# All value matmuls of a sparse attention step in one piece at its end, with five turned tiles kept

## The chip, the cores and the metric

The kernel runs on one core of one Trainium2 chip. The metric is the device time of one execution in microseconds (us). The kernel before takes 2674.22 us (median of 3 runs, 2672.18 to 2682.71).

## What is computed

A decoder trunk of two layers over 512 tokens of width 1024, all in 32-bit floats. What matters here is the middle of each layer, where three branches are mixed; one of them is a sparse attention of 8 heads in 2 groups:

```python
y_a = _conv_module(z_conv, ...) @ conv_out[l]
y_b = _spatial_gating(z_sgu, ...) @ sgu_out[l]
y_c = _nsa(z_q, z_kv, z_ngate, ...) @ nsa_out[l]
g_a, g_b, g_c = jnp.split(jax.nn.sigmoid(z_merge), N_BRANCHES, axis=-1)
h = h + (g_a * y_a + g_b * y_b + g_c * y_c) @ w_out[l]
...
# in _nsa, per block of 128 queries:
p_c = _masked_softmax(s_c, m_c) * m_c          # 31 compressed keys
o_c = jnp.einsum('bghqn,bngd->bqghd', p_c, vc)
p_s = _masked_softmax(s_s, m_s)                # selected blocks
o_s = jnp.einsum('bghqm,bgqmd->bqghd', p_s, vs)
p_w = _masked_softmax(s_w, m_w)                # sliding window
o_w = jnp.einsum('bghqs,bsgd->bqghd', p_w, vw)
return gc[..., 0:1] * o_c + gc[..., 1:2] * o_s + gc[..., 2:3] * o_w
```

With 512 tokens every block is among the selected ones, so the selected and the window part are both plain causal attention over up to 512 keys.

## The kernel before

**Units.** Nearly all work of TensorE (PE) is in *units*: a product of one 1024x128 slice of weights with the 512 tokens, in three matmuls per 128 rows (high by high, high by low, low by high part; lines 706, 709 and 712). ScalarE (ACT) rounds the weights to the high part (`split`, called by `ahead` three units in advance), GpSimd (POOL) makes the low part (line 655), VectorE (DVE) takes the unit's result out of PSUM.

**Attention steps.** The sparse attention has 16 (pair of heads, block of 128 queries) combinations per layer, the *steps* s = 0 to 15. The query blocks of a pair come in the order 3, 0, 2, 1 (`COLS`), so a step sees 512, 128, 384 or 256 keys. Its small matmuls are laid between the matmuls of the merge units. In loop round i (`for i in range(1, NS + 1)`) PE does a branch unit (12 matmuls) and a gate unit (24), and after each second of these 36 matmuls it calls `attention(i, p)` with p = 0 to 17. I call two unit matmuls a *piece*, and a loop round a *round*. In round i these things are issued:

- the scores of step i, `scores((i, 0))` (selected part) and `scores((i, 1))` (window part), both into the same two PSUM banks pS, so the second waits until DVE has taken the first out (semaphore `s_out`);
- the *turned tiles* of step i-1: `turned(i - 1, g)` transposes four 128x128 blocks of probabilities into the one PSUM bank pT; ACT copies it to SBUF (`turned_out`) before the next turned tile may be written (`st_out`). A step has 5, 2, 4 or 3 groups g (`n`), the last of them the 31 compressed keys;
- the value matmuls `values(i - 1, g)`, which read the copied tile and accumulate in pO;
- in rounds 3, 4, 6 and 10 a sum over partitions for a norm (`middle`: q2, mean, var, q3), which uses pT too.

The pieces at which they stand are `TURN_AT`, `VALUE_AT` and `EXTRA_AT`. The turned tiles lie in a ring of two SBUF tiles (`sq`), so that the third copy waits for the value matmuls of the first (semaphore `pv`, line 1495).

**The other engines.** DVE takes scores out of PSUM with a running maximum (`maxes`), ACT makes exponentials (`exps`), DVE the weights (`weigh`), ACT (and from s = 8 partly DVE) multiplies them in (`weighted`); only then may step s be turned (`p_in`). Both engines go strictly in the order written in their own loops over i: ACT from line 1528, DVE from line 2164. In these loops stand also: the square roots of the norms (each needs another table of functions on ACT than the exponential), the copies `pair_high` and `o_st` of finished pairs (rounds 5, 9, 13), the depthwise convolution (`conv`, DVE, rounds 1 to 3) and `late_pair` (DVE, the norm of the next pairs' queries: a reciprocal and a product, at the end of rounds 2, 4 and 10).

Of the kernel before, what the change touches and what calls it, by code (L numbers as in the profile page):

```python
# [17 lines left out]
def trunk(nc, x, mem, norm_ffn1, ffn1_wi, ffn1_wo, norm_mix, w_in, conv_w, conv_b, conv_ln_g,  # L18
# [54 lines left out]
    with ctx:  # L73
# [90 lines left out]
        vt = vtok[:, :, :].rearrange("p a (g c) -> p a g c", g=4)  # L164
        pt = sq

# [25 lines left out]
        NS = PAIRS * TT  # L192
        RING = 2

# [16 lines left out]
        EXTRA = {3: "q2", 4: "mean", 6: "var", 10: "q3"}  # L211
        EXTRA_AT = {3: 4, 4: 4, 6: 5, 10: 3}
        order, seq = ["q1"], []
        for i in range(1, NS + 1):
# [3 lines left out]
            if i in EXTRA:  # L218
                order.append(EXTRA[i])
        TURN_AT = {2: (0, 3), 3: (0, 3, 6), 4: (0, 3, 6, 11), 5: (0, 3, 6, 10, 12)}  # L220
        VALUE_AT = {2: {8: (0, 1)}, 3: {8: (0, 1), 11: (2,)}, 4: {8: (0, 1), 16: (2, 3)},
                    5: {8: (0, 1), 14: (2, 3), 17: (4,)}}
        STEP = {key: n for n, key in enumerate(order)}
# [469 lines left out]
        def _(pe):  # L693
# [145 lines left out]
            for l in range(L):  # L839
# [141 lines left out]
                def values(s, g):  # L981

                    j, c = pair_col(s)
                    n = GRP[s, g]
                    pe.wait_ge(st_out, risen(st_out, l, STEP[s, g] + 1))
                    if n == 0:
                        pe.wait_ge(sg_out, risen(sg_out, l, TT))
                    elif s % TT == 0 and g == 0:

                        if j == 1:  # L990
                            pe.wait_ge(o_st, risen(o_st, l, 1))
                        else:
                            pe.wait_ge(c_l, risen(c_l, l, j))
                    all_of_step = entries(s)
                    for x, (b, k) in enumerate(groups(s)[g]):
                        for e in range(KVG):
                            at = slice((2 * x + e) * P, (2 * x + e + 1) * P)
                            o = pO[e * DH:(e + 1) * DH, c * P:(c + 1) * P]
                            if b < 2:
                                v, p = vt[:, k, 2 * b + e, 0:DH], pt[:, n % RING, at]  # L1000
                            else:
                                v, p = vcs[0:NCMP, e, 0:DH], pt[0:NCMP, n % RING, at]
                            last = mm(o, v, p, start=((b, k) == all_of_step[0]),  # L1003
                                      stop=((b, k) == all_of_step[-1]))
                    last.then_inc(pv, 1)
# [23 lines left out]
                def opening(p):  # L1029
# [10 lines left out]
                    if p == 13:  # L1040
                        scores((0, 1))

                def attention(i, p):
                    n = len(groups(i - 1))
                    if p in TURN_AT[n]:
                        turned(i - 1, TURN_AT[n].index(p))
                    elif i in EXTRA and p == 3 * EXTRA_AT[i]:
                        middle(EXTRA[i], {"q2": 8, "mean": 9, "var": 10, "q3": 11}[EXTRA[i]])
                    elif p in (1, 8):
                        if i < NS:  # L1050
                            scores((i, p // 8))
                    elif p == 16:
                        if i % TT == TT - 1 and f"c{i // TT + 1}" in SLOT:
                            scores(f"c{i // TT + 1}")
                    for g in VALUE_AT[n].get(p, ()):
                        values(i - 1, g)

# [199 lines left out]
        def _(act):  # L1257
# [134 lines left out]
            for l in range(L):  # L1392
# [97 lines left out]
                def turned_out(s, g):  # L1490

                    n = GRP[s, g]
                    act.wait_ge(st_mm, risen(st_mm, l, STEP[s, g] + 1))
                    if n >= RING:
                        act.wait_ge(pv, risen(pv, l, n - RING + 1))
                    rows = P if (s, g) != last_group(s) else NCMP
                    m = 2 * len(groups(s)[g]) * P
                    copy(pt[0:rows, n % RING, 0:m], pT[0:rows, 0:m]).then_inc(st_out, 1)

# [29 lines left out]
                for i in range(1, NS + 1):  # L1529
# [11 lines left out]
                    if i == 13:  # L1541
                        pair_high(2)
                    if i == 8:
                        turned_out(i - 1, 0)
                    ahead(l, branch_unit_of(i - 1))
                    if i != 8:
                        turned_out(i - 1, 0)
                    turned_out(i - 1, 1)
                    if i == 8:
                        conv_high(0)  # L1550
                    if i < NS:
                        exps(i, 0)
                        if i % TT == 0:
                            exps_c(i // TT)
                    if i == 8:
                        conv_high(1)
                    ahead(l, gate_unit(i + 1))
                    for g in range(2, min(n, 4)):
                        turned_out(i - 1, g)
                    if i < NS:  # L1560
                        exps(i, 1)
                    if i == 8:
                        conv_high(2)
                    for g in range(4, n):
                        turned_out(i - 1, g)
# [151 lines left out]
        def _(dve):  # L1717
# [133 lines left out]
            for l in range(L):  # L1851
# [311 lines left out]

                for i in range(1, NS + 1):
                    if i == 9:
                        pair_low(0)
                        pair_low(1)
                    if i == 13:
                        pair_low(2)
                    if i < NS:  # L2170
                        maxes(i, 0)
                    gate(i)
                    if i < 4:
# [222 lines left out]
```

## Time and profile before

| | |
|---|---|
| runs | 2672.18, 2674.22, 2682.71 us |
| the profiled execution | span 2674.3 us, granted TensorE clock 0.997; no time is known around the span |
| PE busy | 2633.2 us (98%) |
| DVE, ACT, POOL busy | 1404.5 us (53%), 1095.5 us (41%), 1230.6 us (46%) |
| rounds 1 to 16, layer 1 | from 553.7 us to 779.2 us of the span; PE 220.3, DVE 128.5, ACT 139.6 busy of 225.5 us |
| rounds 1 to 16, layer 2 | from 1877.9 us to 2104.9 us; PE 221.2, DVE 130.2, ACT 140.5 busy of 227.0 us |
| chain that ended last | PE 63%, issue 17%, POOL 9%, DVE 4%, ACT 3% |

A busy time is a union of the instructions' own spans. Matmuls overlap in the pipeline (one of 512 columns is shown with some 0.39 us and the next starts some 0.23 us later), so what a piece of work costs PE is read from starts to starts, not from durations. In rows of the time line, `[1.14 <-ACT prob L1261]` says that the engine sat idle for 1.14 us before the row, and what ended it.

### The profile page before, as it was taken

Reading aid. Unit: us, or ns where it says so; the run is one execution under the profiler, and the core shown is the slowest. Engines: PE = TensorE matmul, PEld = TensorE weight load, DVE = VectorE, ACT = ScalarE, POOL = GpSimd, SP = SyncE. Lnnn points to the kernel's source line nnn. Section 1 sums busy time; section 2 is a strip of 40 time slices with the busy share of each in tenths; the row PEclk is TensorE's granted clock in tenths of the full one; section 3 lists DMA queues with packets and bytes.
Section 4 is the critical chain, followed back from the end, with each engine's and each line's share of the span. In section 5 each row is a group of like instructions: output and inputs, shape, how many; then the busy total and the mean of one; then the engine's idle time right before and its main releaser. Section 6 shows DMA issues by size and latency. Waiting matters only on the chain.

```text
span 2674.3 us, 35749 instructions
## 1 busy us (share of the span) xinstructions
PE 2633.2 (98%) x12597; PEld 2110.3 (79%) x12597; DVE 1404.5 (53%) x1813; ACT 1095.5 (41%) x1674; POOL 1230.6 (46%) x616
## 2 busy tenths in 40 slices
PE   8999999999999999999999999999999999999999
PEld 6888878866778778888888888887667787788887
DVE  4343458966536544252553535698664364543433
ACT  5322242367644554222342222424675445532222
POOL 4443446762234334444444444477522353444443
PEclk9999999999999999999999999999999999999999
DMA  4334334322233223333333343333222332233332
GB/s 136 102 94 118 102 93 111 75 60 56 60 87 107 79 79 110 95 94 100 89 102 95 95 123 93 105 103 72 60 54 54 99 112 74 87 102 95 100 97 79
DMA packets 474694, 243.75 MB, mean 91 GB/s; under 512 B 41052, under 2 KB 466886, under 8 KB 474566
## 3 DMA queue, kind: packets, MB, share of 16 engines
q1 hardware_dynamic: 474542, 242.04, 32.1%
q8 instruction: 80, 1.31, 0.2%
q14 instruction: 48, 0.39, 0.0%
q10 hardware_dynamic: 24, 0.01, 0.0%
HBM read 237.79 MB, written 2.10 MB: 90 GB/s over the span
## 4 chain that ended last, share of the span: by engine, by line
PE 63%; issue 17%; POOL 9%; DVE 4%; POOLq 3%; ACT 3%; DMA 1%; DVEq 0%; ACTq 0%; SPq 0%
PE pg L706 19%; PE pg L709 18%; PE pg L712 18%; POOL wL L655 8%; PE pA L1003 1%; POOLq L682 1%; PE pA L828 1%; PE pA L950 1%; POOLq L684 1%; PE pg L733 1%; DVE convb L1893 1%; ACT wH L1261 1%; PE pg L1224 1%; PE pg L1222 1%; PE pg L1223 1%
## 5 line engine op out<-in xcount | busy, mean ns | idle before, releaser
L655 POOL TENSOR_TENSOR wL<-raw,wH 128x1024 fp32r<-128x1024 f32 (+1 forms) x472 | 1088.4, 2307 | 1410.2 <-ACT wH L1261 1406.5
L1261 ACT ACTIVATE wH<-raw 128x1024 fp32r<-128x1024 f32 (+1 forms) x472 | 477.6, 1012 | 1124.3 <-PE pg L712 962.5
L706 PE MATMUL pg<-gxH,wH 128*128 128x512 f32 (+1 forms) x2288 | 895.8, 392 | 1.0 <-DVE gxL L1743 0.5
L712 PE MATMUL pg<-gxH,wL 128*128 128x512 f32 (+1 forms) x2288 | 892.2, 390 | 0.0
L709 PE MATMUL pg<-gxL,wH 128*128 128x512 f32 (+1 forms) x2288 | 887.0, 388 | 0.0
L706 PEld LDWEIGHTS pg<-gxH,wH 128*128 128x128 f32 x2288 | 429.9, 188 | 100.2 <-issue 14.7
L712 PEld LDWEIGHTS pg<-gxH,wL 128*128 128x128 f32 x2288 | 429.9, 188 | 89.9 <-issue 4.4
L709 PEld LDWEIGHTS pg<-gxL,wH 128*128 128x128 f32 x2288 | 430.0, 188 | 87.1 <-issue 3.5
L706 PE MATMUL pg<-hH,wH 128*128 128x512 f32 x1008 | 400.0, 397 | 3.1 <-DVE hL L1794 3.1
L712 PE MATMUL pg<-hH,wL 128*128 128x512 f32 x1008 | 399.5, 396 | 0.0
L709 PE MATMUL pg<-hL,wH 128*128 128x512 f32 x1008 | 397.1, 394 | 0.0
L1775 DVE SCALAR_TENSOR_TENSOR xT<-pg,xT 128x512 f32<-128x512 f32 x112 | 77.2, 691 | 358.9 <-PE pg L712 358.6
L1787 DVE TENSOR_TENSOR tmp<-tmp,rstd 128x512 f32<-128x512 f32 x88 | 194.5, 2211 | 117.9 <-ACT tmp L1335 117.9
L1794 DVE TENSOR_TENSOR hL<-tmp,hH 128x512 f32 x88 | 190.2, 2161 | 90.6 <-ACT hH L1261 90.6
L709 PEld LDWEIGHTS pg<-hL,wH 128*128 128x128 f32 x1008 | 189.8, 188 | 51.0 <-issue 12.7
L706 PEld LDWEIGHTS pg<-hH,wH 128*128 128x128 f32 x1008 | 190.4, 189 | 43.0 <-DVE hL L1794 4.8
L712 PEld LDWEIGHTS pg<-hH,wL 128*128 128x128 f32 x1008 | 190.1, 189 | 36.3
L1785 DVE TENSOR_TENSOR tb<-pg,rstd 128x512 f32<-128x512 f32 x88 | 60.7, 690 | 125.4 <-PE pg L712 124.8
L1893 DVE SCALAR_TENSOR_TENSOR pA<-convb,par,pA 128x512 f32<-128x512 f32 x158 | 114.3, 752 | 7.4 <-issue 0.8
L1790 DVE TENSOR_TENSOR tmp<-pg,tmp 128x512 f32<-128x512 f32 x88 | 60.9, 692 | 100.0 <-PE pg L712 97.3
L1261 ACT ACTIVATE sq<-pA 128x512 f32<-128x512 f32 (+1 forms) x112 | 59.1, 528 | 101.4 <-PE pA L828 70.7
L683 POOL TENSOR_TENSOR convb<-convb,wsn 128x512 f32<-128x512 f32 x60 | 84.6, 1411 | 9.1 <-issue 0.4
(271 smaller groups left out, 2232.4 us busy)
## 6 DMA issues: line engine op xcount, KB each, us to landing
raw<-in_ffn_wi SPq DMA_DIRECT2D x352, 256.0 KB, 3.1
raw<-in_w_in SPq DMA_DIRECT2D x200, 256.0 KB, 3.3
raw<-in_ffn_wo SPq DMA_DIRECT2D x128, 256.0 KB, 3.0
raw<-in_ffn_wo SPq DMA_DIRECT2D x64, 192.0 KB, 2.5
raw<-in_xkv SPq DMA_DIRECT2D x32, 256.0 KB, 2.9
raw<-in_w_out SPq DMA_DIRECT2D x32, 256.0 KB, 3.0
raw<-in_sgu_out SPq DMA_DIRECT2D x32, 128.0 KB, 2.3
raw<-in_conv_out SPq DMA_DIRECT2D x32, 128.0 KB, 2.3
```

The lines of the kernel that those rows point to most:

```text
L655: pool.tensor_tensor(wL[:, s % 4, 0:n, :], raw[:, s % 2, 0:n, :], wH[:, s % 4, 0:n, :].bitcast(F32), ALU.subtract)\
L683: pool.tensor_tensor(o, o, term, ALU.add)
L706: mm(o, wH[:, s, k, :], rh(k), start=(k == 0), stop=False)
L709: mm(o, wH[:, s, k, :], rl(k), start=False, stop=False)
L712: last = mm(o, wL[:, s, k, :], rh(k), start=False, stop=(k == kt - 1))
L1261: return act.activation(o, i, ACT.Copy, **kw)
L1775: STT(xT[:, k, :], bank, by, xT[:, k, :], ALU.mult, ALU.add).then_inc(evac, 1)
L1785: TTt(tb[:, 0, :], bank, rstd[:, :], ALU.mult).then_inc(evac, 1)
L1787: TTt(sr, sil, rstd[:, :], ALU.mult)
L1790: TTt(hb, bank, sr, ALU.mult).then_inc(evac, 1)
L1794: TTt(hL[:, slot, :].rearrange(flat), hb, hH[:, slot, :].rearrange(flat).bitcast(F32), ALU.subtract).then_inc(hid_l, 1)
L1893: STT(to, cin[:, j, k:k + T], w, o, ALU.mult, ALU.add)
```

## The change

On PE, `values` of all groups of step i-1 now stand at the last piece (p = 17) of round i. Behind them, in the same piece, stand the first scores of step i+1, in the rounds where i+1 is at least 2 and not 4, 8 or 12 (`FIRST_SCORES_EARLY`); those of step 1 stand in the opening before round 1. In rounds 4, 8 and 12 the first scores stay at p = 1, and the second are at p = 9; in the others the second are at p = 6 (before: 8). The turned tiles stand later, and the extra sums at p = 14 or 11 (before: 12, 12, 15 and 9). The ring of two tiles is replaced by five tiles of their own, of which three are parameter tiles of other parts of the layer (`gbc`, `bbc`, `wsT`). On ACT, `exps(i, 0)` moves ahead of the first turned tile's copy where the first scores are early, and the copies are spread anew around `exps(i, 1)`. On DVE, `maxes(i, 0)` and `gate(i)` move ahead of `pair_low` in rounds 9 and 13.

```diff
-        pt = sq
+        pt = (sq[:, 0, :], sq[:, 1, :], gbc[:, :], bbc[:, :, :].rearrange("p g t -> p (g t)"),
+              wsT[:, :, :].rearrange("p g t -> p (g t)"))
...
-        RING = 2
+        FIRST_SCORES_EARLY = [i for i in range(2, NS) if i % TT]
...
-        EXTRA_AT = {3: 4, 4: 4, 6: 5, 10: 3}
+        EXTRA_AT = {3: 14, 4: 14, 6: 14, 10: 11}
...
-        TURN_AT = {2: (0, 3), 3: (0, 3, 6), 4: (0, 3, 6, 11), 5: (0, 3, 6, 10, 12)}
-        VALUE_AT = {2: {8: (0, 1)}, 3: {8: (0, 1), 11: (2,)}, 4: {8: (0, 1), 16: (2, 3)},
-                    5: {8: (0, 1), 14: (2, 3), 17: (4,)}}
+        TURN_AT = {2: (3, 8), 3: (3, 7, 11), 4: (2, 5, 8, 11), 5: (2, 5, 8, 11, 14)}
...
                     if p == 13:
                         scores((0, 1))
+                    if p == 22:
+                        scores((1, 0))
 
                 def attention(i, p):
                     n = len(groups(i - 1))
                     if p in TURN_AT[n]:
                         turned(i - 1, TURN_AT[n].index(p))
-                    elif i in EXTRA and p == 3 * EXTRA_AT[i]:
+                    elif i in EXTRA and p == EXTRA_AT[i]:
                         middle(EXTRA[i], {"q2": 8, "mean": 9, "var": 10, "q3": 11}[EXTRA[i]])
-                    elif p in (1, 8):
-                        if i < NS:
-                            scores((i, p // 8))
-                    elif p == 16:
-                        if i % TT == TT - 1 and f"c{i // TT + 1}" in SLOT:
-                            scores(f"c{i // TT + 1}")
-                    for g in VALUE_AT[n].get(p, ()):
-                        values(i - 1, g)
+                    elif p == 1 and i < NS and i > 1 and i not in FIRST_SCORES_EARLY:
+                        scores((i, 0))
+                    elif p == (9 if i % TT == 0 else 6) and i < NS:
+                        scores((i, 1))
+                    elif p == 16 and f"c{i // TT + 1}" in SLOT and i % TT == TT - 1:
+                        scores(f"c{i // TT + 1}")
+                    if p == 17:
+                        for g in range(n):
+                            values(i - 1, g)
+                        if i + 1 in FIRST_SCORES_EARLY:
+                            scores((i + 1, 0))
...
-                    if n >= RING:
-                        act.wait_ge(pv, risen(pv, l, n - RING + 1))
+                    if s and g == 0:
+                        act.wait_ge(pv, risen(pv, l, n))
...
-                    if i == 8:
-                        turned_out(i - 1, 0)
                     ahead(l, branch_unit_of(i - 1))
-                    if i != 8:
-                        turned_out(i - 1, 0)
-                    turned_out(i - 1, 1)
+                    if i < NS and i % TT:
+                        exps(i, 0)
+                    turned_out(i - 1, 0)
                     if i == 8:
                         conv_high(0)
-                    if i < NS:
+                    if i < NS and i % TT == 0:
                         exps(i, 0)
-                        if i % TT == 0:
-                            exps_c(i // TT)
+                        exps_c(i // TT)
+                    if n > 2:
+                        turned_out(i - 1, 1)
                     if i == 8:
                         conv_high(1)
                     ahead(l, gate_unit(i + 1))
-                    for g in range(2, min(n, 4)):
+                    for g in range(2 if n > 2 else 1, min(n, 3)):
                         turned_out(i - 1, g)
                     if i < NS:
                         exps(i, 1)
                     if i == 8:
                         conv_high(2)
-                    for g in range(4, n):
+                    for g in range(3, n):
                         turned_out(i - 1, g)
...
                 for i in range(1, NS + 1):
+                    if i < NS:
+                        maxes(i, 0)
+                    gate(i)
                     if i == 9:
                         pair_low(0)
                         pair_low(1)
                     if i == 13:
                         pair_low(2)
-                    if i < NS:
-                        maxes(i, 0)
-                    gate(i)
```

The order on TensorE at the end of round 1, layer 1, before: the value matmuls of step 0 read the ring `sq` and `vtok` (values) or `vcs` (values of the compressed keys). The `kT,qT` row is the second scores of step 1; `ident,pc` is a turned tile.

```order
L950 MATMUL pA<-kT,qT 128x128 x2
L1003 MATMUL pA<-sq,vtok 64x128 x8
...
L828 MATMUL pA<-ident,pc 31x128 x2
...
L1003 MATMUL pA<-sq,vtok 64x128 x8
...
L1003 MATMUL pA<-sq,vcs 64x128 x2
L706 MATMUL pg<-hH,wH 128x512
```

and of the change, the same place (its lines are numbered one less):

```order
L827 MATMUL pA<-ident,pc 31x128 x2
...
L711 MATMUL pg<-gxH,wL 128x512
L1002 MATMUL pA<-sq,vtok 64x128 x8
L1002 MATMUL pA<-gbc,vtok 64x128 x4
L1002 MATMUL pA<-bbc,vtok 64x128 x4
L1002 MATMUL pA<-wsT,vcs 64x128 x2
L949 MATMUL pA<-kT,qT 128x384 x2
L705 MATMUL pg<-hH,wH 128x512
```

Three blocks of value matmuls have become one, and the first scores of step 2 (384 keys) follow it.

The order on ScalarE in round 5, before: `qT<-pA` is the copy `o_st`, `wH<-raw` an `ahead`, `sq<-pA` the copy of a turned tile, `prob,dn<-prob,nb` an exponential of step 5.

```order
L1261 ACTIVATE qT<-pA 128x512
L1261 ACTIVATE wH<-raw 128x1024
L1261 ACTIVATE sq<-pA 128x512 x2
L1477 ACTIVATE prob,dn<-prob,nb 128x128 x2
L1261 ACTIVATE wH<-raw 128x512
L1261 ACTIVATE sq<-pA 128x512 x2
L1477 ACTIVATE prob,dn<-prob,nb 128x128 x2
```

and of the change:

```order
L1265 ACTIVATE qT<-pA 128x512
L1265 ACTIVATE wH<-raw 128x1024
L1481 ACTIVATE prob,dn<-prob,nb 128x128 x2
L1265 ACTIVATE sq<-pA 128x512 x2
L1265 ACTIVATE wH<-raw 128x512
L1265 ACTIVATE gbc<-pA 128x512
L1481 ACTIVATE prob,dn<-prob,nb 128x128 x2
```

The first exponential now stands ahead of the copies of the turned tiles 0 and 1, and the copy of tile 3 has gone behind the second exponential.

## Rows read from the trace of the kernel before

**Rows 1.** Who waited for whom, TensorE, whole run: us, times, longest

```profile
PE pA L828 <- ACT prob L1261: 5.3, 4, 2.0
PE pA L828 <- ACT sq L1261: 5.1, 7, 1.1
```

**Rows 2.** Time line, PE, a score block (at 556.51): start us, us, line

```profile
556.18 0.40 PE L706 MATMUL pg<-hH,wH 128*128 128x512 f32 x1
...
556.93 0.50 PE L709 MATMUL pg<-hL,wH 128*128 128x512 f32 x1
557.27 0.40 PE L712 MATMUL pg<-hH,wL 128*128 128x512 f32 x1
557.50 0.40 PE L706 MATMUL pg<-hH,wH 128*128 128x512 f32 x1
```

**Rows 3.** Time line, PE, scores and eight value matmuls joined

```profile
561.51 0.39 PE L712 MATMUL pg<-gxH,wL 128*128 128x512 f32 x1
...
562.25 1.09 PE L1003 MATMUL pA<-sq,vtok 128*64 128x128 f32 x16
563.27 0.50 PE L706 MATMUL pg<-gxH,wH 128*128 128x512 f32 x1
```

**Rows 4.** Time line, PE, eight value matmuls (566.91), then two alone

```profile
566.58 0.40 PE L712 MATMUL pg<-gxH,wL 128*128 128x512 f32 x1
...
567.93 0.50 PE L706 MATMUL pg<-gxH,wH 128*128 128x512 f32 x1
...
569.19 0.40 PE L712 MATMUL pg<-gxH,wL 128*128 128x512 f32 x1
569.52 0.43 PE L1003 MATMUL pA<-sq,vcs 31*64 31x128 f32 x4
569.88 0.50 PE L706 MATMUL pg<-hH,wH 128*128 128x512 f32 x1
```

**Rows 5.** Time line, round 1 of layer 1: its start, then DVE, then ACT

```profile
553.74 0.39 PE L706 MATMUL pg<-hH,wH 128*128 128x512 f32 x1
...
558.96 0.69 DVE L1727 TENSOR_TENSOR tb<-pg,rstd 128x512 f32<-128x512 f32 x1
...
559.18 0.60 ACT L1261 ACTIVATE sq<-pA 128x512 f32<-128x512 f32 x1 [0.75 <-PE pA L828]
...
559.67 0.39 ACT L1477 ACTIVATE prob<-prob,nb 128x128 f32<-128x128 f32 x1
```

**Rows 6.** Time line, round 5 of layer 1: start, POOL and DVE

```profile
613.73 0.39 PE L706 MATMUL pg<-hH,wH 128*128 128x512 f32 x1
...
615.55 2.40 POOL L655 TENSOR_TENSOR wL<-raw,wH 128x1024 fp32r<-128x1024 f32 x1 [6.10 <-ACT wH L1261]
...
615.95 2.55 DVE L2151 SCALAR_TENSOR_TENSOR qT<-qT,g,rv 128x512 f32<-128x512 f32 x1
...
618.72 0.06 DVE L2058 MEMSET nb<- 128x2 f32 x1 [0.23 <-issue]
```

**Rows 7.** Time line, round 11 of layer 1: start, and DVE

```profile
699.42 0.39 PE L706 MATMUL pg<-hH,wH 128*128 128x512 f32 x1
...
700.74 3.35 DVE L2149 RECIPROCAL rv<-rv 128x512 f32<-128x512 f32 x1 [2.81 <-ACT rv L1571]
...
705.15 0.06 DVE L2058 MEMSET nb<- 128x2 f32 x1 [0.23 <-PE pA L828]
```

**Rows 8.** Time line, rounds 7 and 9: two late turned tiles, a table load

```profile
645.07 0.66 PE L828 MATMUL pA<-ident,prob 128*128 128x128 f32 x4 [0.84 <-ACT sq L1261]
...
646.38 1.28 ACT L1477 ACT_TABLE_LOAD   x1
...
675.06 0.66 PE L828 MATMUL pA<-ident,prob 128*128 128x128 f32 x4 [0.42 <-ACT sq L1261]
```

**Rows 9.** Time line, PE, the longest wait, in layer 2

```profile
1880.52 1.09 PE L828 MATMUL pA<-ident,prob 128*128 128x128 f32 x4 [2.00 <-ACT prob L1261]
```

**Rows 10.** Busy time by stretch: PE, PEld, DVE, ACT, POOL, PEclk, DMA, GB/s

```profile
1880.40:1884.40 4.00, 3.88 (x14) 2.85 (x15) 3.34 (x12) 2.06 (x3) 3.71 (x4) 0.57 0.06 17
```

More of the change, by code:

```diff
@@ L999, in values @@
                             if b < 2:
-                                v, p = vt[:, k, 2 * b + e, 0:DH], pt[:, n % RING, at]
+                                v, p = vt[:, k, 2 * b + e, 0:DH], pt[g][:, at]
                             else:
-                                v, p = vcs[0:NCMP, e, 0:DH], pt[0:NCMP, n % RING, at]
+                                v, p = vcs[0:NCMP, e, 0:DH], pt[g][0:NCMP, at]
                             last = mm(o, v, p, start=((b, k) == all_of_step[0]),
@@ L1493, in turned_out @@
                     act.wait_ge(st_mm, risen(st_mm, l, STEP[s, g] + 1))
-                    if n >= RING:
-                        act.wait_ge(pv, risen(pv, l, n - RING + 1))
+                    if s and g == 0:
+                        act.wait_ge(pv, risen(pv, l, n))
                     rows = P if (s, g) != last_group(s) else NCMP
                     m = 2 * len(groups(s)[g]) * P
-                    copy(pt[0:rows, n % RING, 0:m], pT[0:rows, 0:m]).then_inc(st_out, 1)
+                    copy(pt[g][0:rows, 0:m], pT[0:rows, 0:m]).then_inc(st_out, 1)
                 def pair_high(j):
```

## Prediction, made before the changed kernel ran

> **What bounds the kernel now.** I read the page first: TensorE is busy for 98% of the span, and in the two stretches of sparse attention for 220.3 of 225.5 us and 221.2 of 227.0 us. So what the change is worth is what it does to TensorE's own stream there: what its small blocks cost, and where it stands still. Then I read who TensorE waits for: 11 times for ACT in front of a turned tile, 10.4 us in all [rows 1], four times for the weighted probabilities and seven times for the copy of the tile before. Then the time line, from starts to starts, for the price of a block; and last the time lines of ACT and DVE around the places where the new order puts one thing behind another. ACT and DVE are busy for some 60% of these stretches: they bound nothing by their sums, but both work in a strict order, and TensorE waits for single results.
>
> **Price of the blocks.** Two unit matmuls start 0.23 us apart; a score block of 128 columns makes 0.75 between its neighbours, and the next distance 0.34 [rows 2]. So it costs 0.75 + 0.34 - 2 x 0.23 = 0.63 us. In the same way eight value matmuls alone cost 1.35 + 0.11 - 0.23 = 1.23, and two alone (compressed keys) 0.69 + 0.11 - 0.23 = 0.57 [rows 4]; that is 0.11 per matmul and 0.35 for being a block. Scores and eight value matmuls joined cost 1.76 + 0.11 - 0.23 = 1.64 [rows 3] where apart they would cost 0.63 + 1.23 = 1.86: joining two blocks of unlike shape saves 0.22, of like shape 0.35.
>
> Now the count, per layer. Steps of five tiles (four of them): three value blocks become one, saving 0.35 + 0.22 each, 2.3 in all; the join with scores only changes its side. Steps of three tiles (four): the compressed block is joined, 0.9. Steps of two tiles: all three were joined before, nothing. Steps of four tiles: value blocks are joined, but the joins with the scores (four) and with the compressed scores (three) go, -0.1. Sum 3.1 per layer, **-6.2 us** for both. That scores *behind* values are as cheap as values behind scores no row shows; at 22 places that may be 0.22 more or less each, so -1.4 to -11.
>
> **What goes with the old waits.** In the change every step's first turned tile stands two or three pieces later (0.46 us each), and the second scores in most rounds two pieces earlier, so the weighted probabilities come in time. The waits of [rows 1] go, 10.4 us, and with each some 0.16 more, since the matmul ahead is shown as busy for 0.39 while its successor would start after 0.23: 11 x 0.16 = 1.8. After the wait of 2.00 us [rows 9] the granted clock was 0.57 over 4.0 us [rows 10], TensorE partly at its 1.2 GHz level: 0.43 x 4.0 = 1.7 us of work lost, which goes too. Sum **-13.9 us**. (The ring's waits on ACT, for value matmuls, go as well; no wait of TensorE shows them as its cause.)
>
> **What comes.** The step that decides is on ACT: `exps(i, 0)` now stands ahead of the first copy `turned_out(i-1, 0)`. So the second turned tile, at p = 5 in rounds with four or five tiles, waits not only for the copy, but for all that the first exponential waits for: DVE's `maxes(i, 0)`, and what stands ahead of that on DVE. In the kernel before, the first two copies stood ahead of that exponential, and the second tile waited for the first copy alone. TensorE comes to the second tile six pieces and a turned tile (I take 0.4; four transposes are under the 0.63 of a score block) after the round's start: 6 x 0.46 + 0.4 = 3.2 us. Behind its wait is the whole stream, all units included, so each late tile is a loss in full.
>
> - Round 1. It starts at 553.74 [rows 5], in the change 0.63 later, since the first scores of step 1 have moved ahead of it: 554.4; the second tile is due at 557.6. DVE is without a gap there (it has the norm branch's low parts, the compressed weights and then the convolution to do), so its maximum is done at 558.96 as before [rows 5]; then two exponentials (0.39 each, 0.9 with their sums) and the copy, 0.60 [rows 5]: ready at 560.5. Wait 2.9, before the last tile a second one, since the fourth copy now stands behind `exps(1, 1)`, which waits for DVE's convolution: between 0 and 2, I take 1.2. In layer 2 the first tile is later too (2.00 us of idle time [rows 9]), 0.5 more. Both layers: 8.7.
> - Round 5. DVE begins the maximum at 618.72, behind `late_pair(2)`, 5.0 us after the round's start [rows 6]. Nothing in round 4 frees DVE earlier, and the round begins about where it did (the score block of 0.63 has moved ahead of it, some waits and joins have gone). The maximum takes 0.6, the exponentials 0.9, the copy 0.6: ready 7.1 us after the start, due at 3.2. Wait 3.8, in both layers 7.6.
> - Round 11. ACT's square root for the last queries ends when DVE's reciprocal starts, 1.3 us after the round's start, and the maximum begins at 5.7 [rows 7]. In the change the round's start is later by the score block of 256 keys (about 0.8), the second scores of round 10 stand 0.9 earlier, but the sum q3 0.9 later and on DVE's path: I put the chain 0.9 earlier against the round, maximum at 4.8. With 1.0 for it, 1.1 for the exponentials (256 columns) and 0.6 for the copy: 7.5, due at 3.2. Wait 4.2, both layers 8.4.
> - Round 7. The second tile was 0.84 + 0.16 = 1.0 late, behind the square root [rows 8]. Now the table load of 1.28 [rows 8] and the exponentials (1.1) come ahead of the copy, and the chain is 1.7 earlier against the round (0.8 and 0.9 as above): 1.7, both layers 3.4.
> - Round 9. 0.42 + 0.16 = 0.6 late before [rows 8], behind the copies of finished pairs; now 0.9 more for the exponentials, and 0.2 more because `pair_high(1)` waits for value matmuls that stand at the end of round 8: 1.7, both layers 3.4.
> - Round 3, by the same count (behind `late_pair(1)`): 0.2, both layers 0.4. In rounds 2, 6, 10 and 14 the second tile stands at p = 8, 1.4 later; in rounds 13 and 15 nothing long stands ahead of the maximum, and I count 2.7 to 3.1 against 3.2: nothing, but with little to spare.
>
> Sum **+31.9 us**. Bounds: if ACT's order hid all of it (the exponentials ready at once), 0; if every chain were as late as in the kernel before, with no gain from the earlier scores, some 8 more.
>
> **The clock.** Six of these waits are of 3 us and more (rounds 1, 5, 11, twice). One of 2.00 cost 1.7 us of clock [rows 9, 10]; waits of 1.1 in [rows 1] cost none. I take four falls, **+6.8 us**; bounds 0 and 10.2. The Trainium skill ("TensorE: Matmul & The Clock Gate", HAM oscillation) says that recurring idle stretches throw the engine back to its low clock each time; [rows 9, 10] agree once. By that rule it is six falls and 2696 us.
>
> DVE's product in `late_pair(2)` takes 2.55 us beside POOL's low part [rows 6]; a product of the same size in [rows 5] takes 0.69. The skill ("GPSIMD Engine Reference", Key points) has the two engines share their ways into SBUF, with contention for instructions of two SBUF inputs. The trace agrees; and as ACT's `ahead` starts POOL at the same time in the change, I keep 2.55. Were it free of POOL, 3.7 us less in both layers.
>
> **Sum.** -6.2 - 13.9 + 31.9 + 6.8 = +18.6 us on the profiled execution's span of 2674.3 (0.1 from the median): 2692.9, rounded to **2693 us**. Its own range is 2683 to 2701.
>
> **Rivals.**
> 1. *The order on ACT does not bind* (faster). For it: ACT has 40% idle time, and the first scores are issued at the end of the round before, so that the maximum could be early. Against it: the rows of rounds 5 and 11, where DVE is behind a reciprocal of 3.35. Then there are only the gains, and perhaps 4 us of waits: 2674.3 - 6.2 - 13.9 + 4 = 2658.
> 2. *The new waits are half as long and leave the clock alone* (no change). For it: a round that was delayed gives ACT and DVE time to run ahead in the next. Against: the chains start anew in each round. 2674.3 - 20.1 + 16 = 2670, and up to 2685 with waits of 24 and four falls.
> 3. *More falls and later chains* (slower still): six falls, 8 us more of waits: 2704.
>
> **How the numbers follow.** My forecast 0.50, rival 1 0.13, rival 2 0.29, rival 3 0.08. What a measurement can tell from no change is about 0.5%, 13.4 us: faster is under 2661, slower over 2687.6. Slower: nine tenths of mine and rival 3, 0.53; faster: rival 1, 0.13; same 0.34. The range of eight in ten leaves out most of rival 1 and the far end of rival 3: 2663 to 2703.
>
> **What would show it.** The value matmuls in one row per round, with scores behind them. TensorE's waits for `prob` near 0 except in layer 2's round 1; its waits for the copies (now into `sq`) some 25 us in all, the longest about 4, at the second turned tile of rounds 1, 5, 7, 9 and 11; behind them stretches with a clock under 1. Wrong would be: waits for copies of the size of before, or a clock of 1.00 behind the long ones; or the joined piece costing more than 0.11 per matmul and 0.35 + 0.13 + its scores.

## The result, and the profile after

The changed kernel took 2697.11 us (median of 4 runs, 2693.58 to 2697.84), the kernel before 2674.91 beside it: ratio 1.0073, 95% interval [1.0061, 1.0086]. So it is 22 us slower; forecast were 2693 us. In the profiled executions the spans are 2695.1 and 2674.3 us, 20.8 apart.

Who waited for whom in the changed kernel, TensorE, whole run (us in total, times, longest), against [rows 1]; the copy is line 1265 now, the turned tile 827:

```profile
PE pA L827 <- ACT sq L1265: 27.7, 12, 4.3
...
PE pA L827 <- ACT bbc L1265: 0.3, 1, 0.3
...
PE pA L827 <- ACT prob L1265: 0.2, 1, 0.2
```

The waits for the weighted probabilities (`prob`) are gone but for 0.2 us, and those for the copies (`sq`) are 27.7 us. Where they stand, in layer 1 (time line of TensorE; the number in brackets is the idle time ahead): rounds 1, 5, 7, 9 and 11, each time the second turned tile (one of 0.18 in round 3 is left out):

```profile
560.74 1.11 PE L827 MATMUL pA<-ident,prob 128*128 128x128 f32 x4 [2.90 <-ACT sq L1265]
...
623.59 0.65 PE L827 MATMUL pA<-ident,prob 128*128 128x128 f32 x4 [3.86 <-ACT sq L1265]
...
653.69 0.55 PE L827 MATMUL pA<-ident,prob 128*128 128x128 f32 x3 [1.45 <-ACT sq L1265]
...
682.49 0.55 PE L827 MATMUL pA<-ident,prob 128*128 128x128 f32 x3 [0.73 <-ACT sq L1265]
...
713.85 0.69 PE L827 MATMUL pA<-ident,prob 128*128 128x128 f32 x2 [4.27 <-ACT sq L1265]
```

The chain in front of the longest kind, round 5, which answers to [rows 6] (time line, PE, POOL, DVE and ACT):

```profile
616.24 0.50 PE L705 MATMUL pg<-hH,wH 128*128 128x512 f32 x1
...
618.03 2.38 POOL L654 TENSOR_TENSOR wL<-raw,wH 128x1024 fp32r<-128x1024 f32 x1 [6.35 <-ACT wH L1265]
618.44 2.52 DVE L2154 SCALAR_TENSOR_TENSOR qT<-qT,g,rv 128x512 f32<-128x512 f32 x1
...
621.19 0.06 DVE L2061 MEMSET nb<- 128x2 f32 x1 [0.23 <-issue]
...
621.91 0.40 ACT L1481 ACTIVATE prob<-prob,nb 128x128 f32<-128x128 f32 x1 [3.95 <-DVE nb L2064]
...
622.94 0.60 ACT L1265 ACTIVATE sq<-pA 128x512 f32<-128x512 f32 x1 [0.16 <-issue]
```

Read it backwards from the tile at 623.59: it waits for the copy at 622.94, this stands behind the exponential, which ACT could not start for 3.95 us, since DVE began the maximum at 621.19, behind the product. In the kernel before the two copies were made at 615.38 and 617.27, ahead of all this. The maximum is 4.95 us behind the round's start (5.0 before).

Granted clock, by stretch (columns as in [rows 10]; PEclk is the eighth number, after POOL): six stretches in the attention steps at half clock.

```profile
559.90:566.90 7.00, 6.16 (x21) 4.65 (x22) 6.56 (x11) 2.37 (x6) 6.39 (x5) 0.51 0.14 40
624.90:628.30 3.40, 3.40 (x13) 2.65 (x12) 2.44 (x8) 0.62 (x2) 1.28 (x1) 0.50 0.07 22
713.60:717.00 3.40, 3.15 (x11) 1.86 (x11) 0.00 (x0) 1.31 (x3) 0.81 (x1) 0.50 0.00 0
1894.60:1898.00 3.40, 3.40 (x12) 2.77 (x11) 3.33 (x2) 0.77 (x2) 3.26 (x2) 0.50 0.00 0
1956.10:1959.50 3.40, 3.40 (x12) 2.33 (x11) 1.08 (x6) 1.11 (x2) 1.27 (x1) 0.50 0.00 0
2044.80:2051.60 6.80, 5.60 (x18) 3.80 (x19) 2.13 (x7) 2.11 (x5) 1.26 (x1) 0.50 0.16 46
```

That is 27.3 us with TensorE at its 1.2 GHz level, behind each of the six waits of 2.9 us and more; before it was the one stretch of [rows 10]. Half of such a stretch is lost where TensorE works: 13.7 us, or 12.6 without the 2.2 us in which it stood still anyway, against 1.7 before.

The joined block (round 1's end, against [rows 3, 4]):

```profile
571.04 0.40 PE L711 MATMUL pg<-gxH,wL 128*128 128x512 f32 x1
571.37 1.09 PE L1002 MATMUL pA<-sq,vtok 128*64 128x128 f32 x16
572.29 0.60 PE L1002 MATMUL pA<-gbc,vtok 128*64 128x128 f32 x8
572.73 0.60 PE L1002 MATMUL pA<-bbc,vtok 128*64 128x128 f32 x8
573.26 0.43 PE L1002 MATMUL pA<-wsT,vcs 31*64 31x128 f32 x4
573.63 0.92 PE L949 MATMUL pA<-kT,qT 64*128 64x384 f32 x4
574.47 0.50 PE L705 MATMUL pg<-hH,wH 128*128 128x512 f32 x1
574.81 0.39 PE L708 MATMUL pg<-hL,wH 128*128 128x512 f32 x1
```

By the working of the prediction it costs 3.43 + 0.34 - 2 x 0.23 = 3.31 us.

**A balance for every run.** From each profile I take the span, TensorE's waits of over 0.15 us in the two attention stretches, all time at half clock up to TensorE's last matmul (the last 4 us of a span have none, so a slow clock costs nothing there), and what is left: span - waits - half of the time at half clock. (A wait that lies in a slow stretch is taken off one and a half times; for the changed kernel, three of whose waits reach into a slow stretch by 0.7, 0.3 and 1.2 us, the rest is 1.1 us too low, for the others by 0.7 at most.)

| kernel | median, us | ratio, 95% | span | waits | at half clock (in attention) | rest |
|---|---|---|---|---|---|---|
| before | 2674.91 | 1 | 2674.3 | 10.9 | 13.7 (3.4) | 2656.6 |
| changed | 2697.11 | 1.0073 [1.0061, 1.0086] | 2695.1 | 28.3 | 37.5 (27.3) | 2648.1 |
| second tile later | 2684.15 | 1.0024 [1.0014, 1.0034] | 2682.4 | 16.7 | 30.7 (23.9) | 2650.3 |
| one copy first | 2679.03 | 1.0007 [0.9998, 1.0016] | 2677.3 | 17.7 | 20.5 (10.2) | 2649.4 |
| copies first, rounds 5, 11 | 2678.88 | 1.0014 [1.0005, 1.0024] | 2675.4 | 17.6 | 17.1 (10.2) | 2649.3 |
| two copies first | 2675.32 | 0.9998 [0.9986, 1.0009] | 2676.6 | 16.9 | 23.9 (6.8) | 2647.7 |
| late pairs behind | 2674.32 | 0.9996 [0.9987, 1.0005] | 2672.1 | 14.2 | 13.7 (10.2) | 2651.1 |
| both | 2670.49 | 0.9978 [0.9969, 0.9987] | 2668.4 | 11.3 | 13.7 (6.8) | 2650.3 |
| + fourth copy | 2665.10 | 0.9955 [0.9941, 0.9969] | 2662.4 | 8.4 | 10.2 (0) | 2649.0 |
| values apart | 2673.28 | 0.9980 [0.9970, 0.9991] | 2664.8 | 7.3 | 0 (0) | 2657.6 |
| first scores in their round | 2669.11 | 0.9972 [0.9960, 0.9984] | 2664.0 | 7.7 | 3.4 (0) | 2654.6 |
| scores ahead of values | 2663.41 | 0.9952 [0.9937, 0.9967] | 2658.1 | 7.7 | 0 (0) | 2650.4 |
| convolution later | 2660.99 | 0.9940 [0.9928, 0.9952] | 2656.8 | 3.3 | 10.2 (0) | 2648.4 |

The last column is what to see: 2648 to 2651 wherever the value matmuls are joined with each other and with early scores, 2657 to 2658 where they stand apart, and 2654.6 in the one kernel that joins them but leaves the first scores in their round. The differences beyond that are waits and clock.

### The profile page after: what moved, and what is told of

The parts are those of the page before. It is cut to its first block, busy times and chain, and to the rows that moved or that the text cites. A ratio compares the mean times of both kernels' runs of the same rounds, so it can differ in the third digit from the quotient of the medians.

```text
span 2695.1 us, 35671 instructions
## 1 busy us (share of the span) xinstructions
PE 2637.2 (98%) x12597; PEld 2119.6 (79%) x12597; DVE 1401.6 (52%) x1813; ACT 1096.3 (41%) x1674; POOL 1230.8 (46%) x616
## 4 chain that ended last, share of the span: by engine, by line
PE 63%; issue 17%; POOL 9%; DVE 4%; ACT 3%; POOLq 3%; DVEq 1%; DMA 1%; ACTq 0%; SPq 0%
PE pg L705 18%; PE pg L711 18%; PE pg L708 18%; POOL wL L654 8%; PE pA L827 2%; PE pA L1002 1%; POOLq L681 1%; PE pA L949 1%; POOLq L683 1%; PE pg L732 1%; ACT prob L1481 1%; ACT wH L1265 1%; PE pg L1228 1%; PE pg L1226 1%; PE pg L1227 1%
## 5 line engine op out<-in xcount | busy, mean ns | idle before, releaser
L827 PE MATMUL pA<-ident,prob 128*128 128x128 f32 x416 | 65.5, 284 | 30.6 <-ACT sq L1265 27.7
L827 PEld LDWEIGHTS pA<-ident,prob 128*128 128x128 f32 x416 | 52.6, 146 | 49.2 <-ACT sq L1265 32.8
```

The costliest lines, as they stand in the source:

```text
L827: return pe.transpose(dst, src, ident[0:k, 0:k])
```

## The experiments

All start from the changed kernel; each was timed together with the kernel before, which gave medians of 2675.7 (runs 1 to 4), 2676.1 (5 to 8) and 2677.4 (9 to 11); so the ratios in the table are the surer numbers. In the expectations theory A says that a wait is the end of a strict chain on ACT and DVE less the tile's due time; B, C and D are the rivals named in them.

**1. Two copies first (ACT).** In rounds with first scores early, the edit in short (the line that made the second copy further down leaves it out there):

```diff
-                    if i < NS and i % TT:
-                        exps(i, 0)
                     turned_out(i - 1, 0)
+                    if i < NS and i % TT:
+                        if n > 3:
+                            turned_out(i - 1, 1)
+                        exps(i, 0)
```

> The changed kernel, with ACT's order of the kernel before at one place: in rounds 1 to 15 (without 4, 8, 12) the copies of turned tile 0 (and of tile 1 where there are four or five tiles) stand ahead of exps(i, 0). Theory A (the second turned tile is late because its predecessor's copy stands behind an exponential that waits for DVE): the six waits per layer (27.7 us over the run) go but for some 3 us at later tiles, and the eight 3.4 us windows of half clock in the attention stretches go with them; 2697 - 25 - 13 = 2659 us, faster than the kernel before by 14 to 18. Theory B (it is the joined piece at the round's end that makes ACT and DVE late, whatever their order): the waits stay above 15 us and the time above 2685.

Measured: 2675.32, 22 us better than the changed kernel and level with the kernel before, but 16 short of what I expected. The waits at the second tile are gone but for 0.4 to 0.9 us in round 1. In their place stand two others, one for the copy before the last tile in round 1, one for DVE's eviction in front of the second scores (rounds 5 and 11). Waits of TensorE in layer 1's stretch (the third and fourth copies go into `gbc` and `bbc`):

```profile
PE pA L827 <- ACT bbc L1265: 4.4, 1, 4.4
PE pA L949 <- DVE nb L2069: 2.8, 2, 1.5
PE pA L827 <- ACT sq L1265: 0.4, 1, 0.4
PE pA L827 <- ACT gbc L1265: 0.3, 1, 0.3
```

Their causes, on the time lines of DVE and ACT of the same run, round 1:

```profile
558.95 6.80 DVE L1901 SCALAR_TENSOR_TENSOR convb<-convb,par 128x512 f32<-128x512 f32 x4
...
565.85 0.06 DVE L2066 MEMSET nb<- 128x2 f32 x1
...
566.58 0.40 ACT L1481 ACTIVATE prob<-prob,nb 128x128 f32<-128x128 f32 x1 [5.07 <-DVE nb L2069]
...
567.55 0.60 ACT L1265 ACTIVATE bbc<-pA 128x512 f32<-128x512 f32 x1
...
568.21 0.41 PE L827 MATMUL pA<-ident,pc 128*31 128x128 f32 x2 [4.35 <-ACT bbc L1265]
```

The fourth copy stands behind `exps(1, 1)`, and this behind four steps of DVE's convolution. In the changed kernel TensorE came to the last tile later, held up by its second and at half clock, and the same copy was in time. My expectation had let the late tile vanish and nothing else come due earlier.

**2. One copy first.** As 1, but `exps(i, 0)` directly behind the first copy.

> As e1, but only the copy of turned tile 0 stands ahead of exps(i, 0); that of tile 1 stays behind it. Theory A: the wait moves from the second to the third turned tile, which is due three pieces and a tile later (1.8 us, and in rounds 5 and 11 a score block later still, 2.6): rounds 5 and 11 keep some 1.5 us each per layer, rounds 1, 7 and 9 next to nothing; 2662 to 2668 us. Theory B: as the changed kernel, above 2685.

Measured: 2679.03, 11 above the upper end of what I expected, as run 1 was above its own. The wait that I had put at the third tile of rounds 5 and 11 did not come; the waits are those of run 1, with 0.7 more at the last tile of round 8 in each layer. Near run 1 and not near the changed kernel, so the first copy decides.

**3. Copies first in rounds 5 and 11 alone.**

> As e1, but in rounds 5 and 11 alone. Theory A: the waits of 3.9 and 4.3 us there go in both layers (16.7 us) with the five windows of half clock behind them (8 us), the others stay: 2697 - 25 + 2 = 2674 us, level with the kernel before. Theory B: above 2690.

Measured: 2678.88, 5 above what I expected; waits 17.6 against 28.3, slow stretches 10.2 against 27.3 us. What is left is mostly round 1 (2.9 and 3.1), the eviction, and 1.5 in round 7 of each layer.

**4. The late pairs behind (DVE).** ACT as in the changed kernel, but the reciprocals no longer stand ahead of the maximum:

```diff
-                    if i == 4:
-                        late_pair(2)
 ...
                         squared(1)
+                        late_pair(2)
 ...
                     gate(i)
+                    if i == 11:
+                        late_pair(3)
 ...
-                    if i == 10:
-                        late_pair(3)
```

> The changed kernel, ACT's order untouched; on DVE the query norm late_pair(2) moves from the end of round 4 to the end of round 5, and late_pair(3) from the end of round 10 to behind the gate of round 11, so that the first maximum of rounds 5 and 11 does not stand behind a reciprocal of 3.35 us. Theory A: the wait of round 5 goes (3.9 and 4.3 us), that of round 11 falls from 4.3 to about 1.5, since the square root and the table load on ACT remain; with the clock windows 2697 - 13 - 7 = 2677 us. A rival within A, that ACT itself is late there and not DVE: the waits stay at 3 us or more, 2690 us or more.

Measured: 2674.32. One cause was taken away on another engine, and the same waits went: round 5's wholly, round 11's from 4.27 to 1.10. In layer 1:

```profile
PE pA L827 <- ACT sq L1265: 6.6, 5, 2.9
```

Runs 1 to 4 settle the mechanism: an order on ACT and an order on DVE each bring the same waits or take them away. Theory B, by which these edits would leave the time above 2685, is refuted.

**5. Both.** Runs 1 and 4 together.

> Both edits of the first four runs: the copies of tiles 0 and 1 ahead of exps(i, 0) on ACT, and the two late reciprocals behind the convolution's squares (round 5) and the gate (round 11) on DVE. Theory A (the time is block prices + TensorE's waits + clock falls, and each wait is set by the strict order on ACT or DVE): copies first left 4.35 us at the last tile of round 1 (its copy stands behind exps(1, 1), that behind DVE's convolution) and 1.3 to 1.7 us in front of the second scores of rounds 5 and 11 (DVE evicts the first scores late, behind the reciprocal). The second kind goes, 6.0 us over both layers: 2669. Rival D (the lateness is only moved to the next chain, since DVE has the same work to do): 2675, as copies first alone.

Measured: 2670.49, as theory A had it (2669). The eviction is no longer waited for, and next to nothing has come in its place (one wait of 0.3 a layer).

**6. The fourth copy as well.** In round 1 it stands ahead of `exps(1, 1)`.

```diff
-                    for g in range(2 if n > 2 else 1, min(n, 3)):
+                    third = 4 if i == 1 else 3
+                    for g in range(2 if n > 2 else 1, min(n, third)):
```

> As the run with both edits, and in round 1 the fourth copy (third index) ahead of exps(1, 1) as well. Theory A: the wait of 4.35 us at the last tile of round 1 goes in both layers (8.7) and the two clock falls behind it (2 x 1.7): 2669 - 12 = 2657, faster than the kernel before by 18. Rival D: the last tile or the value matmuls wait for something else in its place, 2667 to 2670.

Measured: 2665.10, so 5 us and not 12. The waits of 4.1 and 4.3 and the slow stretches behind them are gone, but six smaller waits have come. Layer 1:

```profile
PE pA L949 <- DVE nb L2070: 1.6, 1, 1.6
PE pA L827 <- ACT prob L1265: 0.7, 1, 0.7
PE pA L827 <- ACT gbc L1265: 0.6, 2, 0.3
PE pA L827 <- ACT sq L1265: 0.4, 1, 0.4
PE pA L1002 <- ACT wsT L1265: 0.4, 1, 0.4
```

The first two stand in round 2, behind the same convolution. Rival D was half right: DVE's chain was late by itself, and the wait had only covered it. (The time, 2665, lies between theory A's 2657 and rival D's 2667.)

**7. Values apart.** As run 6, with the value matmuls in two or three blocks again:

```diff
+        VALUE_AT = {2: {17: (0, 1)}, 3: {14: (0, 1), 17: (2,)}, 4: {13: (0, 1), 17: (2, 3)},
+                    5: {12: (0, 1), 15: (2, 3), 17: (4,)}}
 ...
-                    if p == 17:
-                        for g in range(n):
-                            values(i - 1, g)
+                    for g in VALUE_AT[n].get(p, ()):
+                        values(i - 1, g)
+                    if p == 17:
```

> As the run with the fourth copy, but the value matmuls stand apart again (pairs 0-1 and 2-3 at pieces 12 and 15 of rounds with five tiles, 13 and 17 with four, 14 and 17 with three; what is left at piece 17). Prices the joining itself. By the blocks' prices as the two traces show them (0.35 per block, 0.2 per join with a block of unlike shape) the joins lost are worth 4.6 us a layer: 9 us above the run with the fourth copy, about 2666. By the prediction's own prices, 5.6 a layer, 11 us above. Rival (joining is worth nothing by itself, only the waits matter): within 2 us of it.

Measured: 2673.28, 8.2 above run 6; by the rests of the two profiles 8.6. Joining is worth what the prices of blocks say, but only where no wait takes it back.

**8. Scores ahead of the values** at a round's end.

```diff
+                        if i + 1 in FIRST_SCORES_EARLY:
+                            scores((i + 1, 0))
                         for g in range(n):
                             values(i - 1, g)
-                        if i + 1 in FIRST_SCORES_EARLY:
-                            scores((i + 1, 0))
```

> As the run with the fourth copy, but at the end of a round the next step's first scores stand ahead of the value matmuls and not behind them. Tells whether the order of the joined shapes has a price: the prediction left 0.22 us at 22 places open to both sides. If not: within 2 us of the run with the fourth copy (the maximum starts up to 3 us earlier, which no wait needs any more). If scores behind values are dear: 5 us faster; if they are cheap: 5 us slower.

Measured: 2663.41, within 2 us of run 6, so scores behind values are neither dear nor cheap. The same block as above, with the order reversed (time line, PE):

```profile
567.87 0.39 PE L711 MATMUL pg<-gxH,wL 128*128 128x512 f32 x1
568.19 0.92 PE L949 MATMUL pA<-kT,qT 64*128 64x384 f32 x4
569.03 1.09 PE L1002 MATMUL pA<-sq,vtok 128*64 128x128 f32 x16
569.96 0.61 PE L1002 MATMUL pA<-gbc,vtok 128*64 128x128 f32 x8
570.39 0.61 PE L1002 MATMUL pA<-bbc,vtok 128*64 128x128 f32 x8
570.93 0.43 PE L1002 MATMUL pA<-wsT,vcs 31*64 31x128 f32 x4
571.30 0.50 PE L705 MATMUL pg<-hH,wH 128*128 128x512 f32 x1
```

From 567.87 to 571.30 are 3.43 us, as in the changed kernel from 571.04 to 574.47: the order has no price. That closes the widest bound of the prediction's first term.

**9. The second tile later (TensorE alone).** ACT and DVE as in the changed kernel:

```diff
-        TURN_AT = {2: (3, 8), 3: (3, 7, 11), 4: (2, 5, 8, 11), 5: (2, 5, 8, 11, 14)}
+        TURN_AT = {2: (3, 8), 3: (3, 7, 11), 4: (2, 8, 11, 13), 5: (2, 8, 10, 12, 14)}
```

> The changed kernel, ACT's and DVE's orders untouched; only TensorE's order moves: in rounds with four or five tiles the second turned tile stands at piece 8 and not 5 (later ones at 11 and 13, or 10, 12 and 14). The wait is the chain's end less the due time, so it must shrink by three pieces, 3 x 0.46 = 1.4 us, where it is longer than that. Theory A: rounds 1, 5, 11 go from 2.9, 3.9 and 4.3 to 1.5, 2.5 and 2.9, round 7 to 0.1, round 9 to 0: 6.4 us a layer, 12.7 in all, and two to four of the eight clock windows: 2697 - 12.7 - 5 = 2679. Rival D (the copies behind each other are the limit; the wait goes over to the third tile, now only two or three pieces behind): 2688 to 2693.

Measured: 2684.15, between theory A's 2679 and rival D's 2688. The waits shrank by 11.6 us, against 12.7 expected, but they are others now; so the single waits that I had put at the second tile (1.5, 2.5 and 2.9) did not come. Layer 1:

```profile
PE pA L949 <- DVE nb L2064: 4.5, 3, 1.9
PE pA L827 <- ACT bbc L1265: 3.9, 1, 3.9
PE pA L1010 <- ACT bbc L1265: 0.5, 1, 0.5
```

The second scores (piece 6) now are the first to meet the late chain of rounds 5 and 11, and in round 1 it is the last tile. And the time at half clock hardly fell, 27.3 to 23.9 us: that is the 5 us that I missed by. The shorter waits at the second scores (1.8 to 2.2 us) were each followed by a slow stretch too.

**10. First scores in their round.** As run 6, with `FIRST_SCORES_EARLY` empty and `scores((1, 0))` at piece 1.

> As the run with the fourth copy, but a step's first scores stand at piece 1 of its own round again, none behind the value matmuls of the round before. Prices the move of the scores. By the blocks' prices 22 joins with the value matmuls are lost, 0.2 each: +4.6 us, and the maxima come 1 us later, for which no tile waits while the copies stand first: 2665 + 5 = 2670. Rival (the early scores matter for the second exponentials and the weighted probabilities, as in the kernel before, which waited four times for them): 2675 and more.

Measured: 2669.11, 4.0 above run 6, in the rests 5.7, where the prices of the joins give 4.6; the rival (2675 and more) does not hold. Behind ACT's repaired order the early scores bring their join and nothing besides.

**11. The convolution later (DVE).** As run 8, and round 1 does two convolution steps at each of two places where it did four; round 3 does the rest.

```diff
                     if i < 4:
-                        conv(4)
+                        conv(4 if i > 1 else 2)
 ...
                         squares(qT[:, 2, :])
-                        conv(4)
+                        conv(2)
```

> As the run with the scores ahead of the values, and four of the convolution's steps that DVE did in round 1 (two ahead of its second maximum, two at its end) are left to round 3. In that run TensorE still waits 1.0 us in round 1 for a copy behind an exponential, and 0.6 and 1.5 us in round 2 for DVE to evict the first scores, behind the convolution. Theory A: the latter go, about 3 us over both layers, little comes back in round 3: 2660. Rival D: round 3's sum over the convolution is late by as much (four steps, 5 us), and the time is the same or worse, 2663 to 2668.

Measured: 2660.99, ratio 0.9940 [0.9928, 0.9952] to the kernel before: the fastest of all, 16 us under the kernel before that was timed beside it and 36 under the changed one. That it is 2.4 under run 8 the times alone do not show (the intervals overlap); the profiles do, with waits of 3.3 us for 7.7. TensorE waits for nothing in round 3: it had room. What TensorE still waits for in layer 1's stretch:

```profile
PE pA L827 <- ACT gbc L1265: 0.9, 3, 0.3
PE pA L827 <- ACT sq L1265: 0.4, 1, 0.4
```

## Why the prediction was right, term by term

- **Blocks: -6.2 forecast, -7.1 measured** (the rest 2656.6 before, 2649.5 as the mean of the nine joined kernels with early scores other than the changed one, 2647.7 to 2651.1; the changed kernel itself, without its 1.1, gives -7.4). So the term is right within what these rests can tell. The bound's cause, a price for scores behind values, is refuted by run 8. One unit has to be read with care: what the prediction calls eight value matmuls are eight of the program, which the trace shows as 16 instructions ([rows 3] say x16), two alone are four; its 0.11 is the price of one of the program's, 0.055 per instruction. The 0.35 for being a block, on which the term rests, is not touched.
- **Old waits and their clock: -13.9 forecast.** The 10.4 us went, but for one wait of 0.25: `prob` is down from 5.3 to 0.2 us, the `sq` waits left are new ones. The slow stretch behind the wait of 2.00 went with it (that wait is the one of 0.25 now). The 0.16 per wait no run shows apart; it comes with each new wait as well.
- **New waits: +31.9 forecast, 28.3 measured as idle time, 30.5 with 0.16 for each of the 14 waits.** Layer 1, forecast and measured idle: round 1 2.9 and 2.90; round 3 0.2 and 0.18; round 5 3.8 and 3.86; round 7 1.7 and 1.45; round 9 1.7 and 0.73; round 11 4.2 and 4.27. In layer 2 round 1 has 3.37 and round 5 4.27, the others are the same. Runs 1, 3 and 4 show ACT's order and DVE's late pair as the causes, from two sides; run 9, in which the same chains meet the second scores instead, agrees. Wrong were the second wait of round 1 (1.2 put, 0.0 and 0.34 measured), where the wait ahead of it had made TensorE late (run 1, without that wait, has 4.35 there), and round 9. Its sum, "now 0.9 more for the exponentials, and 0.2 more because `pair_high(1)` waits", leaves out that the second tile now stands two pieces (0.9 us) later, and ACT has no idle time in front of the copies of `pair_high(1)`. ACT, before and after, at what follows its `ahead`:

```profile
674.42 0.58 ACT L1261 ACTIVATE sq<-pA 128x512 f32<-128x512 f32 x1
...
680.82 0.39 ACT L1481 ACTIVATE prob<-prob,nb 128x128 f32<-128x128 f32 x1
```

  The tile was due at 674.48 then and at 681.60 now (its start less its wait less 0.16), so ACT came to this place 0.06 us ahead of the due time before, and 0.78 ahead of it now.
- **Clock: +6.8 forecast, 13.7 measured in the attention steps** (12.6 of it while TensorE worked). This is the term that failed. The step: four falls at 1.7 each. All six long waits brought a fall, and two of them 6.8 us at half clock instead of 3.4. The Trainium skill ("TensorE: Matmul & The Clock Gate", HAM oscillation) has idle stretches that recur send the engine back to its low clock each time; its own example has waits of some 3 to 5 us. The granted clock of 0.50 to 0.51 at all six waits agrees, and its count of six was better than my four; that waits of 1.8 to 2.2 us are enough, its example does not show, and run 9 does.
- **The sum** was +18.6; measured +22.2 by the medians, +20.8 by the profiles. In the terms of the balance, new less old, forecast and measured: waits +19.7 (31.9 less 12.2) and +17.6 (28.3 less 10.9, and 0.16 for one wait more); half clock +5.1 (6.8 less 1.7) and +10.8 (11.9 less the 1.1 for idle time); blocks -6.2 and -7.4. So the waits were put 2.1 too high and the gain of the blocks 1.2 too small, and against these 3.3 us stands a clock that was put 5.7 too low. Slow stretches outside the attention steps add nothing (10.3 us before, 10.2 after). A total that is off by 2 to 4 us here is partly luck: two errors one way, a larger one the other way.
- **Rival 1** (ACT's order does not bind) is refuted by run 1, **rival 2** (half the waits, clock alone) by the waits themselves. **Rival 3** was right in its falls, wrong in its later chains.
- DVE's product beside POOL took 2.52 us, as the 2.55 of [rows 6]. Here the Trainium skill's "GPSIMD Engine Reference" (Key points) has the two engines share their way into SBUF, with contention, and the trace agrees. The 0.69 that the prediction set beside it is another operation with one input in PSUM; the same product without POOL, in round 11 before, took 0.75:

```profile
704.17 0.75 DVE L2151 SCALAR_TENSOR_TENSOR qT<-qT,g,rv 128x512 f32<-128x512 f32 x1
```

## What to carry to other kernels

Joining blocks on the engine that is the bound pays by the block, and it can be priced in advance from starts; but every move of an operation on the bound engine also moves the due time of what other engines make for it, and a strict order that was free before can then cost more than the join brings. Before such a move, look at each copy that the engine waits for, and at what stands ahead of it in its queue: the short thing that is waited for goes ahead of the long thing that is itself waiting. When a long wait is taken away, ask which chain it had covered; runs 1, 2 and 6 fell short of their expectations mainly for that reason.

## What was not expected of the hardware

- **The clock doubles the price of a wait.** In the attention stretches of all thirteen profiles, with every wait of TensorE of 1.76 us or more there came, within it or at most 1.5 us behind it, a stretch at half clock (24 in all, 19 of 3.4 us and five of 6.8), a loss of 1.7 or 3.4 us. With none of 1.56 us or less did one come, and with one of the five between 1.66 and 1.73 us. So for a wait of 2 us the clock took nearly as much again.
- **The same program falls at different places.** In cross attention, which no edit touched, the time at half clock is between 0 and 17 us from profile to profile. The run with the values apart shows what this makes of one kernel: spans from 2664.8 us at a granted clock of 1.000 to 2674.0 at 0.996. A difference of some us between two single profiles therefore says little until the clock is taken off; that is why the balance above has that column.
- **Unlike shapes cost the same in either order**: 3.43 us for values and then scores, 3.43 for scores and then values.
- **A product on DVE waits for POOL's instruction to end.** The product of `late_pair` (two SBUF inputs) ends 0.55 us behind the low part that POOL was making when it began, however long that was: it took 2.55 and 2.52 us in round 5 before and after, 1.90 in run 4 and 1.20 in run 11, and each time POOL's instruction had ended 0.55 us earlier. Where POOL began 0.2 to 0.4 us behind the product, or not at all, it took 0.75. So its price depends on which of the two starts first, and on how much is left of POOL's work then.
